# The join of two branches and the gathered experts as one stage, with the last norm inside

## The reference, cut to what matters

```
ya  = conv branch @ w_conv_out             # (512 x 1024) @ (1024 x 1024)
yb  = attention output @ w_fox_out
mix = (sigmoid(g_a) * ya + sigmoid(g_b) * yb) @ w_out
x   = x + mix                              # "the join"
h   = rmsnorm(x, norm2_g)
q   = (h @ peer_wq).reshape(T, 8 heads, 256)
s1, s2 = scores of q's two halves against 128 keys each, per head
v1, i1 = top_k(s1, 16); v2, i2 = top_k(s2, 16)
top 16 of the 256 sums v1[i] + v2[j]  ->  16 experts of 16384, gates = softmax
x   = x + sum over 8*16 experts of gelu(u_e . h) * gate_e * v_e
return rmsnorm(x, normf_g)
```

## Time and profile before

| | |
|---|---|
| median of 3 runs | 3682.18 us (3681.05 to 3682.71) |
| profiled execution, span from first to last instruction | 3689.0 us |
| TensorE matmul busy | 3354.4 us (91%) |
| VectorE busy | 2895.0 us (78%) |
| ScalarE busy | 1388.8 us (38%) |
| GpSimd busy | 714.4 us (19%) |
| moved by DMA | 1105.94 MB, mean 300 GB/s |

### The profile page before, as it was taken

How to read it: one execution, slowest core, us unless ns; L and a number is a source line. 1 busy time by engine, 2 the same in 40 slices (tenths; PEclk the granted TensorE clock), 3 DMA queues, 4 the chain that set the end, 5 groups by cost and what they waited for, 6 DMA issues and landing times. The chain is left out here.

```text
span 3689.0 us, 39821 instructions
## 1 busy us (share of the span) xinstructions
PE 3354.4 (91%) x13968; PEld 2302.6 (62%) x13968; DVE 2895.0 (78%) x4727; ACT 1388.8 (38%) x1708; POOL 714.4 (19%) x720
## 2 busy tenths in 40 slices
PE   7999989999999999997999999888888888888876
PEld 5878757878777778774877777644344434334432
DVE  5776579999999999994896464588888888888785
ACT  2244347777777777772233451111111111111111
POOL 0000000000000000001000100144444444444442
PEclk9998989999999999997999999999999999999999
DMA  7421179999999999994324112599999999999997
GB/s 283 142 98 80 28 256 372 377 377 372 382 370 384 371 381 373 380 343 152 101 82 137 46 58 97 227 421 421 417 410 411 416 415 407 421 415 413 417 416 320
DMA packets 253605, 1105.94 MB, mean 300 GB/s; under 512 B 21057, under 2 KB 30657, under 8 KB 187585
## 3 DMA queue, kind: packets, MB, share of 16 engines
q1 hardware_dynamic: 166114, 521.20, 39.0%
q0 software_dynamic: 80640, 562.07, 37.1%
q10 hardware_dynamic: 6720, 20.97, 1.4%
HBM read 1071.15 MB, written 33.03 MB: 299 GB/s over the span
## 5 line engine op out<-in xcount | busy, mean ns | idle before, releaser
L2437 PE MATMUL peer_acc<-peer_rows,peer_diag 128*128 128x512 f32 x2048 | 971.7, 622 | 225.6 <-DVE peer_diag L2586 225.3
L1720 DVE TENSOR_TENSOR moe_w_lo<-ring,moe_w_hi 128x2048 fp32r<-128x2048 f32 x384 | 861.3, 2285 | 36.9 <-ACT moe_w_hi L1636 36.9
L2437 PEld LDWEIGHTS peer_acc<-peer_rows,peer_diag 128*128 128x128 f32 x2048 | 385.0, 197 | 750.0 <-issue 405.4
L1636 ACT ACTIVATE moe_w_hi<-ring 128x2048 fp32r<-128x2048 f32 x384 | 713.8, 1914 | 116.1 <-DMA ring<-in_exp_w 76.6
L2376 POOL DMA_INDIRECT peer_rows<-in_peer_uv,peer_ids x512 | 574.4, 1122 | 922.0 <-PE peer_acc L2437 683.2
L2581 DVE CUSTOM_DVE_ANT_0 peer_rows<-peer_rows,peer_h 128x1024 f32<-128x1024 f32 x512 | 618.4, 1223 | 158.2 <-DMA peer_rows<-in_peer_uv,peer_ids 149.9
L2493 ACT ACTIVATE peer_gelu<-peer_dot 128x2 f32<-128x2 f32 x256 | 52.0, 203 | 1128.1 <-DVE peer_dot L2581 1128.1
L1501 POOL COPY moe_col<-slots 128x1 uint32 (+1 forms) x32 | 53.5, 1672 | 1061.2 <-PE moe_tp L1530 959.4
L2586 DVE TENSOR_SCALAR peer_diag<-consts_sb,peer_gelu,peer_gates 128x128 f32<-128x128 f32 x512 | 162.6, 394 | 68.4 <-ACT peer_gelu L2493 67.3
L1547 PE MATMUL moe_yp<-moe_w_hi,moe_hidt_hi 128*128 128x512 f32 x512 | 168.6, 410 | 2.9 <-DVE moe_hidt_lo L1715 2.9
L241 DVE TENSOR_TENSOR mix_lo<-ring,mix_hi 128x2048 fp32r<-128x2048 f32 (+1 forms) x52 | 116.4, 2252 | 61.5 <-ACT mix_hi L232 61.2
(11 more groups left out here) (473 smaller groups left out, 5798.6 us busy)
## 6 DMA issues: line engine op xcount, KB each, us to landing
ring<-in_exp_w SPq DMA_DIRECT2D x384, 1024.0 KB, 7.3
ring<-in_w_in SPq DMA_DIRECT2D x38, 1024.0 KB, 5.3
y_rows<-moe_y ACTq DMA_DIRECT2D x32, 512.0 KB
z<-in_ada_w SPq DMA_DIRECT2D x12, 1024.0 KB
ring<-in_ada_w SPq DMA_DIRECT2D x4, 2048.0 KB, 14.6
ring<-in_w_out SPq DMA_DIRECT2D x8, 1024.0 KB, 5.0
ring<-in_peer_wq SPq DMA_DIRECT2D x4, 2048.0 KB, 11.2
peer_rows<-in_peer_uv,peer_ids POOLq DMA_INDIRECT x512
```

The lines of the kernel that those rows point to most:

```text
L1636: nc.scalar.activation(w_hi[:, slot, :], env.ring[:, slot, :], ACT.Copy).then_inc(hi_done, 1)
L1720: nc.vector.tensor_tensor(w_lo[:, slot, :], env.ring[:, slot, :], w_hi[:, slot, :].bitcast(F32), ALU.subtract).then_inc(lo_done, 1)
L2437: last = nc.tensor.matmul(acc[:, t % 2, q, :], diag[:, n % SL], rows[:, n % SL, D + q * W:D + (q + 1) * W], start=first, stop=final)
```

## The change

One stage, `join_and_peer`, takes the place of the three.

- The last product is made by token tile. (j0, half 0) still runs over all tiles. After the transposes, tile 0 is finished (both column halves), then tile 1's j0, tile 2's and 3's j0, then j1 for tiles 1, 2 and 3.
- Between these blocks stand tile 0's transposes, the queries and scores of units 0 and 1. Queries 2 and 3 come behind the last block. `keep_busy` before the queries is gone.
- VectorE chooses unit 0 and unit 1 between the additions to `x`. The gathers of experts 0 to 3 may start when unit 0 is chosen, while the product still runs (`rows_a` lies on memory that is free by then); gather 4 waits for the end of the product (`rows_b` lies on `ht3`).
- On ScalarE tile 0's square and root come in the middle of the product. The order after query 3 is as before: squares of tiles 1 to 3 (they wait for all additions), root, exponentials, gelu.
- `peer_wq` is loaded in four parts: the first behind `mixed`, the second behind the second transposes, the last two when piece (j0, half 1) is used.
- The last norm goes tile by tile inside: ScalarE squares tile t - 1 and takes its root after unit (t, head 0); VectorE scales it in unit (t, head 1); SyncE stores it. Only the last tile stands at the end, in two halves of 512 columns, with the root's table loaded beforehand.
- `ht` (transposed h) holds one tile instead of four, `h` two, `pick` lies over constants that are no longer used. Memory is laid out by hand.

```diff
-            tiles.half(pe, ht, 1)
-            tiles.multiply(pe, ht, freed, 4 * NT)
+            w = {(0, 1): pieces.take(pe)}
...
+            mix(0, 1, 0, every).then_inc(done, 1)
+            w[1, 0], w[1, 1] = pieces.take(pe), pieces.take(pe)
+            mix(1, 0, 0, every)
+            mix(1, 1, 0, every).then_inc(done, 1)
+            mix(0, 1, 1, every).then_inc(done, 1)
+            mix(0, 1, 2, fore)
+            turn_tile(0)
+            mix(0, 1, 2, hind).then_inc(done, 1)
+            pe.wait_ge(keys_landed, 16)
+            for side in range(2):
+                query(0, side)
+            mix(0, 1, 3, fore)
+            score(0)
+            mix(0, 1, 3, hind).then_inc(pieces.used, 1)
+            for side in range(2):
+                query(1, side)
+            pe.wait_ge(freed, BRANCHES + 1)
+            mix(1, 0, 1, fore)
+            score(1)
+            mix(1, 0, 1, hind)
+            mix(1, 1, 1, every).then_inc(done, 1)
+            pe.wait_ge(freed, BRANCHES + 3)
+            mix(1, 0, 2, every)
+            mix(1, 1, 2, every).then_inc(done, 1)
+            pe.wait_ge(freed, BRANCHES + 4)
+            mix(1, 0, 3, every).then_inc(pieces.used, 1)
+            mix(1, 1, 3, every).then_inc(pieces.used, 1)
+            for u in range(2, 4):
+                for side in range(2):
+                    query(u, side)
+                if u < 3:
+                    score(u)
+            pe.wait_ge(freed, ALL)
```

ScalarE:

```diff
+            act.wait_ge(freed, BRANCHES + 2)
+            chain(nc.scalar.activation(early_junk[:], env.x[:, 0, :], ACT.Square, accum_out=ms[:, 0:1]))
+            nc.scalar.activation(rstd[:, 0:1], ms[:, 0:1], ACT.Sqrt, bias=eps[:], scale=1.0 / D).then_inc(root, 1)
+            turned_out(0)
+            for u in range(2):
+                query_out(u)
+                score_out(u)
+            query_out(2)
+            score_out(2)
+            query_out(3)
+            act.wait_ge(freed, ALL)
+            for t in range(1, NT):
+                chain(nc.scalar.activation(junk, env.x[:, t, :], ACT.Square, accum_out=ms[:, t:t + 1]))
+            nc.scalar.activation(rstd[:, 1:], ms[:, 1:], ACT.Sqrt, bias=eps[:], scale=1.0 / D).then_inc(root, 1)
+            exp_gates(0)
+            exp_gates(1)
...
+                if head == 0 and t:
+                    square_out(t - 1)
```

VectorE, GpSimd and SyncE:

```diff
+            dve.wait_ge(done, out_done + 4)
+            add_mix(0, 2)
+            choose(0, 0)
+            dve.wait_ge(pieces.used, n_pieces - 2)
+            add_mix(0, 3)
+            for i in range(1, 4):
+                choose(0, i)
+            dve.wait_ge(done, out_done + 5)
+            add_mix(1, 1)
+            for i in range(2):
+                choose(1, i)
+            dve.wait_ge(done, out_done + 6)
+            add_mix(1, 2)
+            for i in range(2, 4):
+                choose(1, i)
+            dve.wait_ge(pieces.used, n_pieces)
+            add_mix(1, 3)
...
+                    if g == 1 and head == 1 and t:
+                        out_scale(t - 1)
+                    if g == 3 and head == 1 and t:
...
+                        out_rows(t - 1, slice(0, D))
...
+                    if n == SL // 2:
+                        pool.wait_ge(pieces.used, n_pieces)
+                    if n >= SL:
+                        pool.wait_ge(v_used, n - SL + 1)
...
+            for t in range(NT - 1):
+                sp.wait_ge(out_ready, t + 1)
+                sp.dma_start(d["out"][t * P:(t + 1) * P, :], env.x[:, t, :]).then_inc(stored, 16)
```

More of the change, by code:

```diff
@@ L2153, in _ @@
                 nc.vector.tensor_tensor(conv[:, c, :], conv[:, c, :], rstd[:], ALU.mult).then_inc(normed, 1)
[L2156 to L2214, removed]
-            tiles.half(pe, ht, 1)
-            tiles.multiply(pe, ht, freed, 4 * NT)
[L2218 to L2270, removed]
-                    nc.vector.tensor_tensor(cut(sgb, t), acc[:, t, :], cut(sgb, t), ALU.mult).then_inc(freed, 1)
-                    dve.wait_ge(freed, (2 + j) * NT + t + 1)
-                    nc.vector.tensor_tensor(cut(sga, t), cut(sga, t), cut(sgb, t), ALU.add).then_inc(mixed, 1)
-                if j == 0:
-                    pieces.split(dve)
-            turned_lo(KC)
-            pieces.split(dve)
-            pieces.split(dve)
-            turned_lo(KC + 4)
-            for j in range(2):
-                for t in range(NT):
-                    tiles.ready(dve, 4 + j, t)
-                    cut = env.x[:, t, j * W:(j + 1) * W]
-                    nc.vector.tensor_tensor(cut, cut, acc[:, t, :], ALU.add).then_inc(freed, 1)
@@ new lines, in join_and_peer @@
+        n_pieces = len(pieces.of_pe) + 8
+        soon = (n_pieces - 4) % RAW // 2
+        ring_slot = lambda i: env.ring[:, 2 * i:2 * i + 2, :].rearrange("p a b -> p (a b)")
+        wq = [wq0, wq1] + [ring_slot(i).rearrange("p (k n) -> p k n", k=KC) for i in (soon, soon + 2)]
+        last_slot = ring_slot(1 - soon)
+        h1, gain_f, junk = (last_slot[:, i * D:(i + 1) * D] for i in range(3))
+        diag = last_slot[:, 3 * D:4 * D].rearrange("p (s n) -> p s n", s=SL)
+        h = lambda t: (h0[:], h1)[t % 2]
@@ new lines, in mix @@
+            def mix(j, half, t, ks):
+                for k in ks:
+                    kk = 4 * half + k
+                    last = product(nc, out_bank(j, t), tuple(a[:, kk, t * P:(t + 1) * P] for a in ht3), tuple(a[:, k, :] for a in w[j, half]),
+                                   kk == 0, kk == KC - 1)
+                return last
+            every, fore, hind = range(4), range(2), range(2, 4)
+            mix(0, 1, 0, every).then_inc(done, 1)
+            w[1, 0], w[1, 1] = pieces.take(pe), pieces.take(pe)
@@ L2436, in _ @@
                         for q in range(2):
-                            last = nc.tensor.matmul(acc[:, t % 2, q, :], diag[:, n % SL], rows[:, n % SL, D + q * W:D + (q + 1) * W],
-                                                    start=first, stop=final)
+                            last = nc.tensor.matmul(sums(t)[:, q, :], diag[:, n % SL], slot(n)[:, D + q * W:D + (q + 1) * W], start=first, stop=final)
                         last.then_inc(v_used, 1)
@@ new lines, in square_out @@
+            def square_out(t):
+                act.wait_ge(x_added, t + 1)
+                chain(nc.scalar.activation(junk, env.x[:, t, :], ACT.Square, accum_out=ms_f[:, t:t + 1]))
+                root_of(t)
+            for q in range(2):
+                nc.scalar.activation(part(conv_hi, q), part(conv, q), ACT.Copy).then_inc(conv_ok, 1)
+                pieces.round(act)
+            act.wait_ge(eps_set, 1)
+            chain(nc.scalar.activation(ms[:, 0:1], eps[:], ACT.Sqrt))
+            rows_out(0)
@@ L2636, in build @@
+            dve.wait_ge(last_squared, 1)
+            chain(nc.vector.tensor_tensor(ms_f[:, last:NT], ms_f[:, last:NT], ms_f[:, NT:NT + 1], ALU.add))
+            dve.sem_inc(last_summed, 1)
+            out_scale(last)
+            for q in range(2):
+                out_rows(last, slice(q * W, (q + 1) * W))
 def build(nc, d):
```

296 lines of the change are left out of this document (201 added, 95 removed).

## The result

The changed kernel takes 3661.83 us (median of 5 runs, 3659.22 to 3664.74) against 3682.18 us (kernel before, 5 runs, 3681.05 to 3682.71): ratio 0.9941, 95% interval 0.9931 to 0.9952, so 0.48 to 0.69% faster. The forecast was 3664, range 3655 to 3672.

A forecast was written before the change was run, and what follows sets the result against it. Gathers were taken as bound by their own transfers, 2.536 us a row. Stream 9.8 plus tail 9.3 less clock 0.6 gave a gain of 18.5, from the median of 3682.2 to 3664; range 3655 to 3672.

The forecast's parts named there:

- Inserts: Last product: tile 0's transposes, two queries and two scores lengthen it by 9.7 us; h is ready 0.3 us before needed.
- First ids and gathers: During the last product: unit 0's ids come at 2340.1, and gathers 0 to 3 are issued from 2340.4.
- The list on ScalarE sets gather 8: Start of the gathers: gather 8 waits through matmul, diag and gelu for ScalarE's in-order work; diag 2367.9, gather 8 2372.3.
- A pause of 8.6 us: Behind the first eight gathers: transfers stand still from 2365.5 to 2374.1, until gather 8's data.
- early gathers that buy nothing: Gathers 0 to 3 during the product: without them eight rows would end at 2374.2, the same.
- The stream: Gathers of all rows: 504 rows at 2.536 us from 2374.1 plus 3.8 end at 3656.0 instead of 3665.8, gain 9.8.
- the clock's dip: At the inserted transposes: one dip of the granted clock would cost 1.2 to 1.7 us; 0.6 taken off the gain.
- the stores: Three stores of 0.5 MiB inside the gathers cost 3.8 us at the rows' pace, possibly as little as 0.
- The tail: From last dot product to span's end: 13.85 us instead of 23.15, gain 9.3, bounds 8 and 10.3.
- the rival with the clock: Transposes to query 3: TensorE at 1.2 instead of 2.4 GHz, 39 us become 78, 3703; chance 0.03.
- The cover at tile ends: Three tile ends: ScalarE's extra 2.85 us each costs 0, as engines can be 10 us late; 8.6 without it.
- The missing pause: Rival at the start of the gathers: rows 4 on flow from 2354.0 without a stop, 3653; chance 0.08.

The follow-up runs named there:

- squares_late: Changed kernel with ScalarE's squares of tiles 1 to 3 and their root moved behind unit 0's last gelu; 3656.37 us, ratio 0.9931.
- spread_list: Changed kernel with query 3 in halves behind matmul groups 1 and 2, squares behind gelus, first gelu ahead of query 2's copy; 3652.19 us; also run with late stores, 3646.97.
- no_early: Changed kernel with gathers 0 to 3 also waiting for the end of the last product, like gather 4; 3661.05 us, ratio 0.9945.
- after_again: The changed kernel run once more, unedited, as reference; 3661.03 us, ratio 0.9945.
- norm_outside: Changed kernel with all four tiles' last norm and stores put behind the last addition, in the same stage; 3667.66 us, ratio 0.996.
- squares_six: Changed kernel with ScalarE making its square six times instead of once at each of three tile ends; 3665.53 us, ratio 0.9953.
- short_list: Changed kernel with squares and root late, first exponentials ahead of query 2's copy, query 3 behind unit 0's first matmuls; 3657.71 us, ratio 0.9933.
- inserts_behind: Changed kernel with tile 0's transposes, queries, scores and the choices of units 0 and 1 behind the whole last product; 3669.9 us, ratio 0.9964.
- short_list_stores: short_list with the stores of tiles 0 to 2 also waiting until the last gather has landed; 3659.21 us, ratio 0.9933.
- stores_late: Changed kernel with the stores of tiles 0 to 2 waiting until the last gather has landed; 3655.14 us, ratio 0.9927.

## Why the prediction was right, point by point

- **Inserts** (term: 9.7 us). Measured 8.9; the transposes, queries and scores stand back to back, with no wait for h. The 0.3 us to spare held: h is done at 2310.85, the first transpose starts at 2311.15.
- **First ids and gathers** (2340.1 and 2340.4, that is 28.8 after the first addition). Gather 0 at 28.3.
- **The list on ScalarE sets gather 8** (forecast: diag 56.3, gather 8 60.7 after the first addition). Measured 55.5 and 60.1. Shown by squares_late, which shortens it by a known amount and passes that on undiminished, and by spread_list.
- **A pause of 8.6 us** and early gathers that buy nothing. The windows have 8 us; no_early has the same median. Right, and removing the pause in spread_list is worth 8.2.
- **The stream.** 9.8 less 0.6 us of gain forecast; last dot 11.9 us earlier in the count. The difference of 2.7 has small terms in it that all went one way: the clock's dip that did not come (0.6), the inserts (0.8) and the stores (3.0 instead of 3.8). Each is under what two runs of one kernel differ by, so the split is a likely one and not shown; in after_again the last dot is another 1.0 earlier. That the terms did not cancel means that the forecast's closeness, 2 us off the median, owes little to luck.
- **The tail** (9.3 us). Measured 9.8. norm_outside splits it into 8.1 and 1.7.
- **Clock.** The granted clock was 1.00 in every window from 2303 to 2351 of the changed kernel, transposes and queries included. So the 0.6 taken off was too much and the rival with the clock did not happen. The Trainium skill (TensorE: Matmul & The Clock Gate, "PE-mode transpose") does not count transposes as busy; eight of them in 0.8 us between matmuls did not matter here.
- **The cover at tile ends** (term: 0) came out, but it was thinner than said. The prediction worked out 10 us from the distance of a gather's issue to its dot at the end of the program, and set ScalarE's 2.85 us of new work against all of it. squares_six shows that the distance between two issues may reach about 9 us before the stream loses, so the size is nearly right; but it is not all spare. The changed kernel already has 4.0 to 4.8 us between these issues at a tile end, and a late gelu lets TensorE's clock fall, which adds 1 to 2 us. What was free was some 5 us at the gathers. The changed kernel stays under it: its longest wait for a gelu is 2.2 us, as before.
- **The missing pause** was priced at 3653 as a rival, and spread_list, where it is gone, has 3652.19. This nearness is luck. The rival's sum lies 10.5 us off the forecast's, since it leaves out the 0.5 MiB of gain_f (1.3 us) and the 0.6 for the clock, which the forecast's sum has; the pause alone was 8.6 there, and spread_list measures 8.2, from a kernel that was itself 2 to 3 us quicker than forecast.
- **A slip in a reading** without weight: the last slice of the earlier trace rows has 7 and 320 GB/s, and not 9 and over 407; it holds the tail.

## What to carry to other kernels

A stage bound by its transfers gains only by when the stream starts, whether it ever runs dry and what else rides in it. So before moving work ahead of such a stream, write down for the first transfer that must wait for a buffer everything it waits for, on every engine, in order: here it was one engine's list behind two queries, and the early transfers went into its shadow. When an item is taken off that list, look at once at what stands second: short_list moved the same pause by one gelu.

Stores in a full stream cost 2.4 to 3.1 us here where the rows' pace would give 3.8; let them wait for the drain at the end where there is one. The depth of a queue isn't all spare: take off the pause between issues that the work already has at that place, and what an engine takes longer when it starts again.

## What the runs showed of the hardware that was not expected

The same code had different granted clocks in the stretch from 270 to 330 us, and the fourteen profiled runs fall into three groups: 0.81 or 0.82 (before, inserts_behind, short_list_stores), with the join's first load at 2187.9 to 2189.7 us; 0.91 (the changed kernel's run and five more), with the load at 2179.5 to 2182.0; and 1.00 (after_again, no_early, stores_late and both spread_list runs), with the load at 2177.2 to 2180.1. Between the first group and the others lie 6 to 13 us, a third to more than half of what this change is worth, and they come from outside of it. The clock and the lateness go together; that the one makes the other, and what decides it, was not tried. Between spans of single profiles nothing of this size can be read, and counting from a common event repeated to 1.0 us.

Writes of 1.5 MiB amid gathers cost 3.0, 2.4, 3.0 and 3.1 us in four pairs of runs, less each time than the 3.8 us of the same bytes as gathered rows at 2.536 us a MiB.
